# Gate and up products of an expert issued as one pass over two column groups each

## The chip, the cores and the metric

The kernel runs on one core of a Trainium2 chip. TensorE (PE) multiplies, ScalarE (ACT) and VectorE (DVE) do the elementwise work, GpSimd (POOL) helps at the start, and SyncE (SP) issues the transfers, which 16 DMA engines carry out. The metric is the time of one launch on the device, in microseconds (us): the median of the runs, where lower is better.

## The reference

A decoder trunk of two layers on 256 tokens of width 1024, all in float32. Each layer has a mixer (attention and a gated recurrence in layer 0, sliding-window attention in layer 1) and after it a mixture of 32 experts, two of them chosen for each token. The change touches the experts alone, whose arithmetic is:

```python
def expert_block(args):
    xblk, e = args
    hid = jax.nn.silu(xblk @ w_gate[e]) * (xblk @ w_up[e])
    return hid @ w_down[e]
```

`w_gate[e]` and `w_up[e]` are 1024x512, `w_down[e]` is 512x1024: 2 MB each, 6 MB an expert, and every expert's weights are read once in each layer.

## The kernel before

Weights come in chunks of 2 MB (128 partitions x 4096 floats), three to an expert: gate, up, down. Four experts are a quad, so a quad is 12 chunks and a layer 8 quads. The code of a layer's experts is in three pieces: a first quad (`quad(..., first=True)`), a loop over `quad`, and `last_quad`. If more than 32 tokens choose one expert, the loop runs again over all quads.

SBUF has 11 buffers for chunks, seven in `ring` and four in `side`; one of them serves chunk 5 and chunk 11 of a quad. SyncE goes through the chunks in a fixed order (`again`, L357): for each it waits until the chunk that had the buffer has been used (`chunk_done`, which TensorE counts up by one when a product has read its chunk) and then issues the transfer. The last chunk of a layer comes in four pieces (`last_in_pieces`, L387). The queue is first in, first out: later chunks stand behind earlier ones. The mixer's work needs the same buffers, so only the first chunks of a layer's experts are there when its routing ends; the rest start as the first expert gives buffers back (the first chunk's buffer even in three parts, L395).

TensorE works through a quad in one order. It gathers the tokens of the four experts (L989, in the last quad L1169) into `gatherT`, 32 columns an expert. For each expert it then runs the gate product and after it the up product (L1025, in the last quad L1181): the 32 columns of tokens are the stationary operand, the weights move past in four pieces of 128 columns, and the four pieces go to four groups of 32 columns of the array, which run at the same time. So gate lands as 128 partitions x 128 columns of a PSUM bank and up as the next 128 columns. One matmul in float32 is two matmul and two weight-load instructions in the profile: a gate product is 32 matmuls and stands there as x64.

ScalarE waits until gate and up are both done (`products_done(layer, i, 3 * e + 1)` waits for the up chunk) and takes SiLU of the gate part into SBUF (L1556, in the last quad L1568); VectorE multiplies it by the up part (L1656); TensorE turns the result (L1040, L1193); VectorE copies it to SBUF as `hidT` (L2179, L2204); and TensorE runs the down product (L1060, L1202), four steps over `hidT` in four column groups of 256 columns each, x32 in the profile. ScalarE and VectorE copy its result out (L1560 and L2183, L1576).

After a quad TensorE combines the results into the tokens (L1068). In the last quad the combination is done expert by expert (L1092: that of expert 0 stands behind expert 1's up product, that of expert 1 behind expert 2's up product, that of expert 2 behind expert 2's down product), and the fourth expert is followed in small pieces: its gate product, copies of x into PSUM (L1102 in layer 1, L1108 in layer 0), its up product, the rest of these copies, and its down product piece by piece (L1121) as the pieces of the last chunk land.

Of the kernel before, what the change touches and what calls it, by code (L numbers as in the profile page):

```python
# [15 lines left out]
P = 128  # L16
S = 256
TT = S // P
D = 1024
KD = D // P  # L20
# [10 lines left out]
CAP = 32  # L31
QE = 4
# [64 lines left out]
def build(nc, weights, small, table, x_in, xT_in, out):  # L97
# [3 lines left out]
    with ctx:  # L101
# [27 lines left out]
        at = 0  # L129
# [58 lines left out]
        yq = probT[:, 1, :]  # L188
        scr6 = scr[:, :].rearrange("p (b a c) -> p b a c", b=6, a=2)
        silu, hid, hidT = scr6[:, 0, :, :], scr6[:, 1, :, :], scr6[:, 2, :, :]  # L190
        pick, pickw = scr6[:, 3, :, :], scr6[:, 4, :, :]
        pickT = scr[:, 5 * S:6 * S]

# [21 lines left out]
        def last_sums(h, j):  # L215

            return PS[:, LAST[j]:LAST[j] + 2, h * S:(h + 1) * S].rearrange("p j (a n) -> p a j n", a=TT)

        def buffer(n):

# [8 lines left out]
        ident = tb("id")  # L229
# [310 lines left out]
        def _(pe):  # L540
# [461 lines left out]
            def turn_weights(i, layer, bank):  # L1002
# [3 lines left out]
                    tr = pe.transpose(PS[:, bank, t * P:(t + 1) * P], pickw[:, t, :], ident)  # L1006
                tr.then_inc(m_pickw_turned, 1)

            def quad(layer, i, first=False):

                if first:
                    gather_rest(i, layer)
                else:
                    gather(i, layer)
                for e in range(QE):
                    b = 2 + e % 2
                    tok = slice(e * CAP, (e + 1) * CAP)

                    for up in range(2):
                        w = cols(moe_landed(layer, i, 3 * e + up, first))  # L1020
                        for k in range(KD):
                            if e == 0 and up == 0 and k % 4 == 0:
                                pe.wait_ge(m_gatherT, 2 * i + 1 + k // 4)
                            for f in range(4):
                                mm = pe.matmul(PS[f * CAP:(f + 1) * CAP, b, up * P:(up + 1) * P],  # L1025
                                               gatherT[:, k, tok], w[:, k, f * P:(f + 1) * P],
                                               start=(k == 0), stop=(k == KD - 1))
                            if first and e == 0 and up == 0 and k in (1, 3):
                                mm.then_inc(part_read, 1)
                        mm.then_inc(chunk_done, 1)  # L1030
                        if first and e == 0 and up == 0:
                            for t in range(TT):
                                mm = pe.matmul(PS[:, 7, 64:96], tb("ones"), rt[:, 0, t, :], start=(t == 0),
                                               stop=(t == 1))
                            mm.then_inc(counted, 1)
                    if first and e == 0:
                        turn_weights(i, layer, 3)
                        pe.wait_ge(m_pickT, i + 1)
                    pe.wait_ge(m_hid, QE * i + e + 1)
                    pe.transpose(PS[:, b, 2 * P:3 * P], hid[:, e % 2, :], ident).then_inc(m_hid_turned, 1)  # L1040
                    w = halves(moe_landed(layer, i, 3 * e + 2))
                    early = first and e == QE - 1
                    if early:
                        pe.wait_ge(half_landed, 16 * (layer + 1))
                        w0 = spare.rearrange("p (f n) -> p f n", f=4)
                        pe.wait_ge(more_landed, 16 * (layer + 1))

                    def part(f, q):

                        at = f * 512 + q % 2 * 256  # L1050
                        if early and q < 2:
                            return w0[:, f, q * 256:(q + 1) * 256]
                        if early and at < MORE[layer]:
                            return more(layer)[:, at:at + 256]
                        return w[:, q // 2, f, q % 2 * 256:(q % 2 + 1) * 256]

                    pe.wait_ge(m_hidT, QE * i + e + 1)
                    for f in range(4):
                        for q in range(4):
                            mm = pe.matmul(PS[q * CAP:(q + 1) * CAP, e % 2, 0:256],  # L1060
                                           hidT[:, e % 2, f * CAP:(f + 1) * CAP], part(f, q),
                                           start=(f == 0), stop=(f == 3))
                    mm.then_inc(chunk_done, 1)

                pe.wait_ge(m_y, 2 * QE * i + 2 * QE)
                for t in range(TT):
                    for q in range(4):
                        pe.matmul(PS[:, OUT[q], t * 256:(t + 1) * 256], pickT[:, t * P:(t + 1) * P],  # L1068
                                  yq[:, q * 256:(q + 1) * 256], start=(first and t == 0), stop=False,
                                  skip_group_check=True)  # L1070
# [91 lines left out]
            def last_quad(layer, i):  # L1162
# [9 lines left out]
                for e in range(QE):  # L1172
                    b = 2 + e % 2
                    tok = slice(e * CAP, (e + 1) * CAP)
                    for up in range(2):
                        w = cols(moe_landed(layer, i, 3 * e + up))
                        for k in range(KD):
                            if e == 0 and up == 0 and k % 4 == 0:
# [10 lines left out]
                        turn_picks(i)  # L1189
                    elif e < QE - 1:  # L1190
                        combine(i, e - 1)
                    pe.wait_ge(m_hid, QE * i + e + 1)
                    pe.transpose(PS[:, b, 2 * P:3 * P], hid[:, e % 2, :], ident).then_inc(m_hid_turned, 1)  # L1193
                    if e == 0:
                        pe.wait_ge(m_pickT, i + 1)
                    if e == QE - 1:
# [3 lines left out]
                    for f in range(4):  # L1200
                        for q in range(4):
                            mm = pe.matmul(PS[q * CAP:(q + 1) * CAP, e % 2, 0:256],  # L1202
                                           hidT[:, e % 2, f * CAP:(f + 1) * CAP],
                                           w[:, q // 2, f, q % 2 * 256:(q % 2 + 1) * 256],
                                           start=(f == 0), stop=(f == 3))
                    mm.then_inc(chunk_done, 1)
# [90 lines left out]
        def _(act):  # L1297
# [251 lines left out]
                act.wait_ge(chunk_done, DONE_MOE[layer] + j + 1 + QC * i)  # L1549

            def quad(layer, i, weights_bank=2):
                act.wait_ge(m_pickw_turned, i + 1)
                act.activation(pickT[:, :], PS[:, weights_bank, 0:S], ACT.Copy).then_inc(m_pickT, 1)
                for e in range(QE):
                    products_done(layer, i, 3 * e + 1)
                    act.activation(silu[:, e % 2, :], PS[:, 2 + e % 2, 0:P], ACT.Silu).then_inc(m_silu, 1)  # L1556

                    products_done(layer, i, 3 * e + 2)
                    for q in range(2):
# [4 lines left out]
            def last_quad(layer, i):  # L1564

                for e in range(QE):
                    products_done(layer, i, 3 * e + 1)
                    act.activation(silu[:, e % 2, :], PS[:, 2 + e % 2, 0:P], ACT.Silu).then_inc(m_silu, 1)  # L1568
                    if e == 0:
                        act.wait_ge(m_pickw_turned, i + 1)  # L1570
                        act.activation(pickR[:, 0:2, :].rearrange("p e t -> p (e t)"), PS[:, 0, :], ACT.Copy)
# [74 lines left out]
        def _(dve):  # L1646
# [517 lines left out]
            def quad(layer, i, build=None):  # L2164
# [9 lines left out]
                for e in range(QE):  # L2174
                    b = 2 + e % 2
                    dve.wait_ge(m_silu, QE * i + e + 1)
                    tt(hid[:, e % 2, :], silu[:, e % 2, :], PS[:, b, P:2 * P], ALU.mult).then_inc(m_hid, 1)
                    dve.wait_ge(m_hid_turned, QE * i + e + 1)
                    dve.tensor_copy(hidT[:, e % 2, :], PS[:, b, 2 * P:3 * P]).then_inc(m_hidT, 1)  # L2179

# [6 lines left out]
            def last_quad(layer, i):  # L2187
# [5 lines left out]
                for e in range(QE):  # L2193
# [5 lines left out]
                            tt(xs, xs, PS[:, OUT[q], :].rearrange("p (a n) -> p a n", a=TT),  # L2199
                               ALU.add).then_inc(part_acc, 1)  # L2200
                    dve.wait_ge(m_silu, QE * i + e + 1)
                    tt(hid[:, e % 2, :], silu[:, e % 2, :], PS[:, b, P:2 * P], ALU.mult).then_inc(m_hid, 1)
                    dve.wait_ge(m_hid_turned, QE * i + e + 1)
                    dve.tensor_copy(hidT[:, e % 2, :], PS[:, b, 2 * P:3 * P]).then_inc(m_hidT, 1)  # L2204
                for h in range(2):
# [180 lines left out]
```

## Time and profile before

| | us |
|---|---|
| runs | 1134.91, 1135.9, 1137.19 (median 1135.9) |
| profiled execution | 1138.64 |
| its span | 1136.8 |
| TensorE busy in it | 870.0 (77%) |
| VectorE / ScalarE busy | 300.2 / 186.5 |
| mean granted TensorE clock | 0.907 |

The span is from the first to the last instruction of the profiled execution, and 1.84 us of its time lie outside it. That execution took 2.7 us more than the median run. In the profile's 40 slices the experts of layer 0 fill about slices 7 to 21 and those of layer 1 slices 25 to 40; before and between them are the mixers.

### The profile page before, as it was taken

To read this page: it belongs to the slowest core of one execution; us is meant where nothing else is said; L and a number is where in the kernel's file an instruction comes from. 1 tells how busy PE (TensorE), PEld (TensorE's weight loads), DVE (VectorE), ACT (ScalarE), POOL (GpSimd) and SP (SyncE) were. 2 spreads that over 40 slices of the span, in tenths; PEclk is the share of its full clock that TensorE was granted. 3 is DMA by queue.
4 is the path that set the end of the run, shared out by engine and by line. 5 is a ranking of instruction groups with operands and counts; after the bars stand their busy time and mean duration, and the time that the engine had idled before them with its cause. 6 is when DMAs were issued, how large, how long until landed. Compare 5 with 4: busy or idle time off the path is not lost.

```text
span 1136.8 us, 28905 instructions
## 1 busy us (share of the span) xinstructions
PE 870.0 (77%) x12910; PEld 639.2 (56%) x12910; DVE 300.2 (26%) x959; ACT 186.5 (16%) x495; POOL 25.7 (2%) x29
## 2 busy tenths in 40 slices
PE   7999998787575757575779999787776757666666
PEld 6665647676464545454547457576664545444545
DVE  3566735122111111111103774221211111111101
ACT  4323532110000000000003452011100000000000
POOL 1221000000000000000000000000000000000000
PEclk9999999999888879888889999899988888888898
DMA  9955458999999999999999777999999999999997
GB/s 378 430 218 218 164 206 327 416 429 427 432 432 431 429 434 429 429 432 432 427 430 426 302 286 275 381 428 426 432 432 428 432 432 429 431 432 428 431 428 308
DMA packets 34732, 440.91 MB, mean 388 GB/s; under 512 B 3952, under 2 KB 4080, under 8 KB 8048
## 3 DMA queue, kind: packets, MB, share of 16 engines
q1 hardware_dynamic: 34384, 439.89, 92.3%
q8 instruction: 47, 0.77, 0.3%
q10 hardware_dynamic: 288, 0.15, 0.0%
q14 instruction: 13, 0.11, 0.0%
HBM read 438.97 MB, written 1.05 MB: 387 GB/s over the span
## 4 chain that ended last, share of the span: by engine, by line
DMA 52%; PE 37%; DVE 5%; ACT 2%; issue 2%; SPq 1%; DVEq 0%; another core or an unknown queue 0%; ACTq 0%
DMA side<-weights 43%; PE PS L580 9%; DMA ring<-weights 9%; PE PS L1060 8%; PE PS L1025 6%; PE PS L754 1%; PE PS L921 1%; PE PS L590 1%; PE PS L1068 1%; PE PS L989 1%; DVE scr L1656 1%; SPq L357 1%; PE PS L1181 1%; PE PS L665 1%; DVE side L1902 1%
## 5 line engine op out<-in xcount | busy, mean ns | idle before, releaser
L1025 PE MATMUL PS<-ring,probT 128*32 128x128 f32 x4480 | 150.7, 294 | 47.7 <-DMA ring<-weights 43.4
L1025 PEld LDWEIGHTS PS<-ring,probT 128*32 128x32 f32 x4480 | 134.4, 119 | 62.3 <-DMA ring<-weights 51.7
L1025 PE MATMUL PS<-side,probT 128*32 128x128 f32 x2688 | 105.5, 322 | 69.0 <-DMA side<-weights 66.0
L1025 PEld LDWEIGHTS PS<-side,probT 128*32 128x32 f32 x2688 | 92.3, 131 | 88.2 <-DMA side<-weights 81.7
L580 PE MATMUL PS<-ring,side 128*128 128x512 f32 (+1 forms) x320 | 136.2, 575 | 0.3 <-DVE side L1940 0.3
L1656 DVE TENSOR_TENSOR scr<-scr,PS 128x128 f32<-128x128 f32 x64 | 18.5, 288 | 384.9 <-ACT scr L1556 317.4
L580 PEld LDWEIGHTS PS<-ring,side 128*128 128x128 f32 x320 | 58.8, 190 | 61.0 <-issue 59.8
L2183 DVE COPY probT<-PS 32x256 f32<-32x256 f32 x112 | 47.5, 424 | 171.6 <-PE PS L1060 170.8
L1060 PE MATMUL PS<-side,scr 128*32 128x256 f32 x842 | 66.3, 462 | 25.6 <-DMA side<-weights 21.8
L1060 PE MATMUL PS<-ring,scr 128*32 128x256 f32 x896 | 69.1, 460 | 21.9 <-DMA ring<-weights 12.4
L1560 ACT ACTIVATE probT<-PS 32x256 f32<-32x256 f32 x112 | 41.8, 373 | 231.9 <-PE PS L1060 231.3
L1556 ACT ACTIVATE scr<-PS 128x128 f32<-128x128 f32 x56 | 15.5, 277 | 344.7 <-PE PS L1025 344.7
L1068 PE MATMUL PS<-probT,scr 128*128 128x256 f32 x224 | 57.6, 415 | 13.8 <-DVE probT L2183 13.8
L1068 PEld LDWEIGHTS PS<-probT,scr 128*128 128x128 f32 x224 | 45.4, 208 | 30.2 <-DVE probT L2183 23.5
L1060 PEld LDWEIGHTS PS<-ring,scr 128*32 128x32 f32 x896 | 34.7, 127 | 44.7 <-issue 22.1
L1060 PEld LDWEIGHTS PS<-side,scr 128*32 128x32 f32 x842 | 31.3, 127 | 49.0 <-DMA side<-weights 26.7
L1040 PE MATMUL PS<-TB,scr 128*128 128x128 f32 x56 | 19.1, 342 | 42.4 <-DVE scr L1656 42.4
L1656 DVE TENSOR_TENSOR probT<-PS,SM 128x512 f32<-128x512 f32 (+1 forms) x36 | 23.8, 662 | 103.7 <-PE PS L989 88.5
L989 PE MATMUL PS<-scr,x 128*128 128x128 f32 x384 | 46.8, 275 | 0.0
L989 PEld LDWEIGHTS PS<-scr,x 128*128 128x128 f32 x384 | 45.7, 192 | 0.6
L1040 PEld LDWEIGHTS PS<-TB,scr 128*128 128x128 f32 x56 | 8.0, 143 | 59.0 <-DVE scr L1656 56.9
L1181 PE MATMUL PS<-ring,probT 128*32 128x128 f32 x640 | 20.8, 286 | 6.2 <-DMA ring<-weights 5.8
(286 smaller groups left out, 822.1 us busy)
## 6 DMA issues: line engine op xcount, KB each, us to landing
ring<-weights SPq DMA_DIRECT2D x124, 2048.0 KB, 34.1
side<-weights SPq DMA_DIRECT2D x74, 2048.0 KB, 26.9
side<-weights SPq DMA_DIRECT2D x6, 1024.0 KB, 10.2
ring<-weights SPq DMA_DIRECT2D x10, 512.0 KB, 7.3
xn<-weights SPq DMA_DIRECT2D x2, 1024.0 KB, 6.8
ring<-weights SPq DMA_DIRECT2D x2, 1024.0 KB, 8.3
side<-weights SPq DMA_DIRECT2D x5, 256.0 KB, 26.8
xn<-xT_in SPq DMA_DIRECT2D x2, 512.0 KB, 5.5
```

Of the source, the lines that this page charges most:

```text
L357: return sp.dma_start(buffer(slot), source).then_inc(w_landed[slot], 16)
L580: mm = pe.matmul(PS[:, bank, 0:n], hT[:, k, t * P:(t + 1) * P], w[:, k, 0:n], start=(k == 0), stop=(k == KD - 1))
L989: mm = pe.matmul(PS[:, half, k * P:(k + 1) * P], x[:, t, d * P:(d + 1) * P], pick[:, t, :], start=(t == 0), stop=(t == TT - 1))
L1025: mm = pe.matmul(PS[f * CAP:(f + 1) * CAP, b, up * P:(up + 1) * P], gatherT[:, k, tok], w[:, k, f * P:(f + 1) * P], start=(k == 0), stop=( ...
L1040: pe.transpose(PS[:, b, 2 * P:3 * P], hid[:, e % 2, :], ident).then_inc(m_hid_turned, 1)
L1060: mm = pe.matmul(PS[q * CAP:(q + 1) * CAP, e % 2, 0:256], hidT[:, e % 2, f * CAP:(f + 1) * CAP], part(f, q), start=(f == 0), stop=(f == 3))
L1068: pe.matmul(PS[:, OUT[q], t * 256:(t + 1) * 256], pickT[:, t * P:(t + 1) * P], yq[:, q * 256:(q + 1) * 256], start=(first and t == 0), sto ...
L1181: mm = pe.matmul(PS[f * CAP:(f + 1) * CAP, b, up * P:(up + 1) * P], gatherT[:, k, tok], w[:, k, f * P:(f + 1) * P], start=(k == 0), stop=( ...
L1556: act.activation(silu[:, e % 2, :], PS[:, 2 + e % 2, 0:P], ACT.Silu).then_inc(m_silu, 1)
L1560: ins = act.activation(yq[e * CAP:(e + 1) * CAP, q * 256:(q + 1) * 256], PS[q * CAP:(q + 1) * CAP, e % 2, 0:256], ACT.Copy)
L1656: return dve.tensor_tensor(o, a, b, op)
L2183: ins = dve.tensor_copy(yq[e * CAP:(e + 1) * CAP, q * 256:(q + 1) * 256], PS[q * CAP:(q + 1) * CAP, e % 2, 0:256])
```

## The change

An expert's gate and up product become one pass (`gate_up`). The stationary operand and the order over the eight k steps are as before, but a k step has four matmuls of 256 columns in place of eight of 128: gate's 512 columns go to column groups 0 and 1, up's to groups 2 and 3. So the pass waits for both chunks before its first matmul, gate's result lies on partitions 0 to 63 and up's on partitions 64 to 127, each 256 columns wide, and `chunk_done` goes up by two at the end of the pass. SiLU and the multiplication then work on 64 partitions x 256 columns instead of 128x128, the result stands on partitions 64 to 127 (`act_up`), and it is turned by two ordinary matmuls against a 64x64 identity instead of one transpose; the down product reads its four blocks in another order (`hid_rows`). The first expert of a layer's first quad and the last of its last quad keep the old form.

```diff
@@ tiles
+        act_up = scr6[2 * CAP:P, 0:2, :, :].rearrange("p a b c -> p (a b c)").rearrange("p (e n) -> p e n", e=2)
...
+        def hid_rows(f, pair):
+
+            at = (f % 2 * 2 + f // 2 if pair else f) * CAP
+            return slice(at, at + CAP)
...
@@ TensorE
+            def gate_up(layer, i, e, first=False):
+
+                b = 2 + e % 2
+                w = [cols(moe_landed(layer, i, 3 * e + up, first)) for up in range(2)]
+                for k in range(KD):
+                    if e == 0 and k % 4 == 0:
+                        pe.wait_ge(m_gatherT, 2 * i + 1 + k // 4)
+                    for q in range(4):
+                        mm = pe.matmul(PS[q * CAP:(q + 1) * CAP, b, 0:S], gatherT[:, k, e * CAP:(e + 1) * CAP],
+                                       w[q // 2][:, k, q % 2 * S:(q % 2 + 1) * S], start=(k == 0), stop=(k == KD - 1))
+                mm.then_inc(chunk_done, 2)
+
+            def turn_hidden(i, e):
+
+                b = 2 + e % 2
+                pe.wait_ge(m_hid, QE * i + e + 1)
+                for c in range(2):
+                    tr = pe.matmul(PS[:, b, 2 * P + c * 2 * CAP:2 * P + (c + 1) * 2 * CAP],
+                                   act_up[:, e % 2, c * P:(c + 1) * P], ident[2 * CAP:P, 2 * CAP:P],
+                                   start=True, stop=True)
+                tr.then_inc(m_hid_turned, 1)
...
@@ quad, for every expert
-                    for up in range(2):
+                    pair = not (first and e == 0)
+                    if pair:
+                        gate_up(layer, i, e, first)
+                    for up in range(0 if pair else 2):
...
-                    pe.wait_ge(m_hid, QE * i + e + 1)
-                    pe.transpose(PS[:, b, 2 * P:3 * P], hid[:, e % 2, :], ident).then_inc(m_hid_turned, 1)
+                    if pair:
+                        turn_hidden(i, e)
+                    else:
+                        pe.wait_ge(m_hid, QE * i + e + 1)
+                        pe.transpose(PS[:, b, 2 * P:3 * P], hid[:, e % 2, :], ident).then_inc(m_hid_turned, 1)
...
-                                           hidT[:, e % 2, f * CAP:(f + 1) * CAP], part(f, q),
+                                           hidT[:, e % 2, hid_rows(f, pair)], part(f, q),
...
@@ last_quad
-                    for up in range(2):
+                    pair = e < QE - 1
+                    if pair:
+                        gate_up(layer, i, e)
+                    for up in range(0 if pair else 2):
...
@@ ScalarE, quad (last_quad the same, with e == QE - 1 for the old form)
-                    act.activation(silu[:, e % 2, :], PS[:, 2 + e % 2, 0:P], ACT.Silu).then_inc(m_silu, 1)
+                    if first and e == 0:
+                        act.activation(silu[:, e % 2, :], PS[:, 2 + e % 2, 0:P], ACT.Silu).then_inc(m_silu, 1)
+                    else:
+                        act.activation(act_up[:, e % 2, :], PS[0:2 * CAP, 2 + e % 2, 0:S], ACT.Silu).then_inc(m_silu, 1)
...
@@ VectorE, quad (last_quad the same, with e == QE - 1 for the old form)
-                    tt(hid[:, e % 2, :], silu[:, e % 2, :], PS[:, b, P:2 * P], ALU.mult).then_inc(m_hid, 1)
+                    if build is not None and e == 0:
+                        tt(hid[:, e % 2, :], silu[:, e % 2, :], PS[:, b, P:2 * P], ALU.mult).then_inc(m_hid, 1)
+                    else:
+                        tt(act_up[:, e % 2, :], act_up[:, e % 2, :], PS[2 * CAP:P, b, 0:S], ALU.mult).then_inc(m_hid, 1)
```

TensorE in layer 1's last quad, before, from the wait for expert 2's gate chunk to expert 3's gate product. L561 is the wait for a chunk, L1181 the gate and up products, L1089 and L1192 waits, L1092 the combination, L1193 the turn of the hidden block, L1202 the down product:

```order
L561 REGISTER_ALU
L1181 MATMUL PS<-side,probT 32x128 x32
L561 REGISTER_ALU
L1181 MATMUL PS<-ring,probT 32x128 x32
L1089 REGISTER_ALU
L1092 MATMUL PS<-probT,TB 128x256 x8
L1192 REGISTER_ALU
L1193 MATMUL PS<-TB,scr 128x128
L1202 MATMUL PS<-ring,scr 32x256 x16
L1089 REGISTER_ALU
L1092 MATMUL PS<-probT,TB 128x256 x8
L1181 MATMUL PS<-side,probT 32x128 x32
```

The same place now. The two chunk waits stand together at L567, L1023 is the pass over both chunks (the first two of its 16 alternating rows open the first piece, the last two the second), L1126 the combination, L1032 the turn, L1242 the down product, L1218 expert 3's gate product:

```order
L567 REGISTER_ALU x2
L1023 MATMUL PS<-side,probT 32x256 x2
L1023 MATMUL PS<-ring,probT 32x256 x2
```

```order
L1023 MATMUL PS<-side,probT 32x256 x2
L1023 MATMUL PS<-ring,probT 32x256 x2
L1123 REGISTER_ALU
L1126 MATMUL PS<-probT,TB 128x256 x8
L1030 REGISTER_ALU
L1032 MATMUL PS<-TB,scr 128x64 x2
L1242 MATMUL PS<-ring,scr 32x256 x16
L1123 REGISTER_ALU
L1126 MATMUL PS<-probT,TB 128x256 x8
L1218 MATMUL PS<-side,probT 32x128 x32
```

Expert 2's gate product has moved behind the wait for its up chunk; what follows, the combination, the turn, the down product and expert 3, stands in the order it had.

ScalarE in the last quad, before, from expert 2's SiLU to expert 3's (L1568 is the SiLU, L1549 and L1582 wait for products, L1576 copies out a down product):

```order
L1568 ACTIVATE scr<-PS 128x128 [waits chunk_done]
L1549 REGISTER_ALU
L1576 ACTIVATE probT<-PS 128x256 [waits chunk_done]
L1549 REGISTER_ALU
L1568 ACTIVATE scr<-PS 128x128 [waits chunk_done]
L1582 ACTIVATE probT<-PS 128x128 [waits down_half_done]
```

And now (L1615 is the SiLU of the new form, L1613 that of the old):

```order
L1615 ACTIVATE scr<-PS 64x256 [waits chunk_done]
L1589 REGISTER_ALU
L1623 ACTIVATE probT<-PS 128x256 [waits chunk_done]
L1589 REGISTER_ALU
L1613 ACTIVATE scr<-PS 128x128 [waits chunk_done]
L1629 ACTIVATE probT<-PS 128x128 [waits down_half_done]
```

Nothing has moved there; the SiLU of experts 0 to 2 has another shape, and it waited for both products before as well.

## Rows read from the trace of the kernel before

**Rows 1.** The page, busy tenths of the DMA engines in 40 slices
```profile
DMA  9955458999999999999999777999999999999997
```

**Rows 2.** Steady stretches: busy us of each engine (instructions), PEclk, DMA share, GB/s
```profile
262.00:550.00 288.00, 193.47 (x3482) 148.16 (x3478) 41.38 (x110) 22.37 (x65) 0.00 (x0) 0.85 1.01 430
812.00:1070.00 258.00, 168.89 (x3066) 128.36 (x3066) 35.96 (x96) 19.93 (x58) 0.00 (x0) 0.85 1.01 431
```

**Rows 3.** The page, transfers of chunks: count, KB each, median us to landing
```profile
ring<-weights SPq DMA_DIRECT2D x124, 2048.0 KB, 34.1
```

**Rows 4.** TensorE's timeline, layer 0's first quad: start, us, operation
```profile
198.93 3.68 PE L1025 MATMUL PS<-ring,probT 128*32 128x128 f32 x128
```

**Rows 5.** Transfers issued in 198:199.9, and in 200:202: us to landing
```profile
ring<-weights SPq DMA_DIRECT2D x1, 2048.0 KB, 9.1
...
ring<-weights SPq DMA_DIRECT2D x1, 2048.0 KB, 12.3
```

**Rows 6.** SyncE's timeline in layer 1's second quad
```profile
771.51 0.33 SPq L357 DMA_DIRECT2D side<-weights  x1
```

**Rows 7.** The transfer issued in 771.4:771.9: us to landing
```profile
side<-weights SPq DMA_DIRECT2D x1, 2048.0 KB, 11.1
```

**Rows 8.** TensorE's timeline at the end of layer 1
```profile
1105.72 2.73 PE L1181 MATMUL PS<-side,probT 128*32 128x128 f32 x64 [4.33 <-DMA side<-weights]
1110.63 3.35 PE L1181 MATMUL PS<-ring,probT 128*32 128x128 f32 x64 [2.18 <-DMA ring<-weights]
1113.92 1.15 PE L1092 MATMUL PS<-probT,TB 32*128 32x256 f32 x16
1115.80 1.93 PE L1202 MATMUL PS<-ring,scr 128*32 128x256 f32 x32 [0.47 <-DVE scr L2204]
1118.57 1.15 PE L1092 MATMUL PS<-probT,TB 32*128 32x256 f32 x16 [0.83 <-ACT probT L1576]
1120.35 1.96 PE L1181 MATMUL PS<-side,probT 128*32 128x128 f32 x64 [0.63 <-DMA side<-weights]
1122.23 2.86 PE L1102 MATMUL PS<-x,TB 128*128 128x256 f32 x12
1125.18 1.96 PE L1181 MATMUL PS<-side,probT 128*32 128x128 f32 x64
```

**Rows 9.** Weight loads of TensorE there, expert 3's up product
```profile
1125.18 1.69 PEld L1181 LDWEIGHTS PS<-side,probT 128*32 128x32 f32 x64 [0.50 <-DMA side<-weights]
```

**Rows 10.** TensorE's timeline at the end of layer 0
```profile
588.23 1.95 PE L1181 MATMUL PS<-ring,probT 128*32 128x128 f32 x64 [1.24 <-DMA ring<-weights]
...
593.11 1.93 PE L1202 MATMUL PS<-ring,scr 128*32 128x256 f32 x32 [1.59 <-DMA ring<-weights]
...
597.94 3.50 PE L1181 MATMUL PS<-side,probT 128*32 128x128 f32 x64 [1.19 <-DMA side<-weights]
...
604.32 1.96 PE L1181 MATMUL PS<-side,probT 128*32 128x128 f32 x64
```

**Rows 11.** Single microseconds with TensorE's clock, columns as in rows 2
```profile
1112.00:1113.00 1.00, 1.00 (x27) 0.92 (x23) 0.00 (x0) 0.00 (x0) 0.00 (x0) 0.50 0.88 377
```

**Rows 12.** The same in layer 1's first quad
```profile
735.00:736.00 1.00, 1.00 (x22) 0.85 (x14) 0.00 (x0) 0.00 (x0) 0.00 (x0) 0.50 1.11 461
...
740.00:741.00 1.00, 1.00 (x16) 0.53 (x12) 0.00 (x0) 0.00 (x0) 0.00 (x0) 0.50 0.92 393
```

**Rows 13.** Groups by form: count, busy us, mean ns of one, idle before
```profile
L1656 DVE TENSOR_TENSOR scr<-scr,PS 128x128 f32<-128x128 f32 x64 | 18.5, 288 | 384.9 <-ACT scr L1556 317.4 <-ACT scr L1568 67.3
...
L1556 ACT ACTIVATE scr<-PS 128x128 f32<-128x128 f32 x56 | 15.5, 277 | 344.7 <-PE PS L1025 344.7
...
L1656 DVE TENSOR_TENSOR scr<-scr,wexp 128x256 f32<-128x256 f32 x16 | 6.7, 420 | 0.1
...
L1553 ACT ACTIVATE scr<-PS 128x256 f32<-128x256 f32 x14 | 5.4, 383 | 89.3 <-PE PS L1006 89.3
```

**Rows 14.** TensorE's waits over the span: us in total, times, longest
```profile
PE PS L1025 <- issue: 7.2, 5, 2.4
```

More of the change, by code:

```diff
@@ L1191, in last_quad @@
                         combine(i, e - 1)
-                    pe.wait_ge(m_hid, QE * i + e + 1)
-                    pe.transpose(PS[:, b, 2 * P:3 * P], hid[:, e % 2, :], ident).then_inc(m_hid_turned, 1)
+                    if pair:
+                        turn_hidden(i, e)
+                    else:
+                        pe.wait_ge(m_hid, QE * i + e + 1)
+                        pe.transpose(PS[:, b, 2 * P:3 * P], hid[:, e % 2, :], ident).then_inc(m_hid_turned, 1)
                     if e == 0:
@@ L1202, in last_quad @@
                             mm = pe.matmul(PS[q * CAP:(q + 1) * CAP, e % 2, 0:256],
-                                           hidT[:, e % 2, f * CAP:(f + 1) * CAP],
+                                           hidT[:, e % 2, hid_rows(f, pair)],
                                            w[:, q // 2, f, q % 2 * 256:(q % 2 + 1) * 256],
@@ L1551, in quad @@
             def quad(layer, i, weights_bank=2):
+                first = weights_bank == 3
                 act.wait_ge(m_pickw_turned, i + 1)
@@ L1567, in last_quad @@
                     products_done(layer, i, 3 * e + 1)
-                    act.activation(silu[:, e % 2, :], PS[:, 2 + e % 2, 0:P], ACT.Silu).then_inc(m_silu, 1)
+                    if e == QE - 1:
+                        act.activation(silu[:, e % 2, :], PS[:, 2 + e % 2, 0:P], ACT.Silu).then_inc(m_silu, 1)
+                    else:
+                        act.activation(act_up[:, e % 2, :], PS[0:2 * CAP, 2 + e % 2, 0:S], ACT.Silu).then_inc(m_silu, 1)
                     if e == 0:
@@ L2176, in quad @@
                     dve.wait_ge(m_silu, QE * i + e + 1)
-                    tt(hid[:, e % 2, :], silu[:, e % 2, :], PS[:, b, P:2 * P], ALU.mult).then_inc(m_hid, 1)
+                    if build is not None and e == 0:
+                        tt(hid[:, e % 2, :], silu[:, e % 2, :], PS[:, b, P:2 * P], ALU.mult).then_inc(m_hid, 1)
+                    else:
+                        tt(act_up[:, e % 2, :], act_up[:, e % 2, :], PS[2 * CAP:P, b, 0:S], ALU.mult).then_inc(m_hid, 1)
                     dve.wait_ge(m_hid_turned, QE * i + e + 1)
@@ L2201, in last_quad @@
                     dve.wait_ge(m_silu, QE * i + e + 1)
-                    tt(hid[:, e % 2, :], silu[:, e % 2, :], PS[:, b, P:2 * P], ALU.mult).then_inc(m_hid, 1)
+                    if e == QE - 1:
+                        tt(hid[:, e % 2, :], silu[:, e % 2, :], PS[:, b, P:2 * P], ALU.mult).then_inc(m_hid, 1)
+                    else:
+                        tt(act_up[:, e % 2, :], act_up[:, e % 2, :], PS[2 * CAP:P, b, 0:S], ALU.mult).then_inc(m_hid, 1)
                     dve.wait_ge(m_hid_turned, QE * i + e + 1)
```

## The prediction

> **What bounds the kernel now.** I read first the 40 slices of the page, then the two long stretches of the experts, then the transfers, and last TensorE's timeline at the places where a layer's experts begin and end. The DMA row [rows 1] shows 9 in nearly all slices of the experts and gaps only in the mixers. The stretches say the same with a number: DMA share 1.01 at 430 GB/s, while TensorE is busy 193.47 of 288.00 us (67%) and 168.89 of 258.00 us (65%) [rows 2]. A chunk of 2 MB (2.1 million bytes) takes 4.9 us of such a stream, and an expert's three chunks 14.6 us. A chunk is issued 34.1 us before it lands [rows 3], so about seven chunks are in the queue. In the steady stretches the time is that of the stream, and TensorE waits for landings.
>
> So three places can matter: the start of a layer's experts, where the queue is short; the end, where nothing is left to load; and anything that would empty the queue between.
>
> At the end of layer 1 the reader is to see where the waits stop. Expert 2's gate product waits 4.33 us for its chunk, its up product 2.18 us, expert 3's gate product still 0.63 us, and from 1120.35 on TensorE goes from one operation to the next [rows 8]. Expert 3's up product starts at 1125.18, and its weight loads name the landing of its chunk as what they waited for [rows 9], while TensorE came free only at 1122.23 + 2.86 = 1125.09: both arrive within 0.1 us. There is no slack behind expert 3's gate product, so whatever delays it there delays the end of the span by as much.
>
> **The pass itself.** Removed per pair: 128 matmul instructions of 128 columns. Added: 64 of 256 columns. The old pair runs in 3.68 us when both chunks are there [rows 4]. The nearest row for the new form is the down product, which also has 256 columns in each of four groups: 32 instructions in 1.93 us [rows 8], so 64 in at most 3.86. Bounds 3.4 (below the old pair, should the many instructions have cost something) to 3.9; I take 3.7. No TensorE work is saved, the columns are the same.
>
> The Trainium skill (TensorE: Matmul & The Clock Gate, "Wait — 56ns, not 53.3ns?") puts a floor of about 25 ns under each matmul and 2.5 ns on each at full clock. By an estimate from it, 64 instructions fewer would save under 0.2 us of a pair. Rows 4 show 3.68 us / 128 = 29 ns an instruction, near that floor, and rows 8 1.93 / 32 = 60 ns for twice the columns, so the trace shows no such saving.
>
> **What the pair moves.** The gate product no longer runs in the 4.9 us in which the up chunk lands. After the up chunk's landing there are now 3.7 us of work at full clock where there were 1.95. And the clock is not full then. After the waits of this place the granted clock is 0.50 (1.2 of 2.4 GHz) [rows 11], and expert 2's up product takes 3.35 us instead of 1.95 [rows 8]; in layer 0 expert 3's gate product takes 3.50 [rows 10]. TensorE came free of expert 1 at 1105.72 - 4.33 = 1101.4; with expert 1's own pass some 2 us later, it will be idle for about 7 us up to 1110.63, so the pass starts slow. Bounds: 3.7 (full clock) and 7.4 (slow throughout; the clock stayed at 0.50 from 735 to 741 with TensorE mostly busy [rows 12]). A slow stretch in rows 8 and 10 costs one product 1.4 to 1.55 us, so I take one such loss, rounded up for the higher share of slow work: 5.4 us.
>
> **The path behind it, at the end of layer 1.**
> - Expert 2's pass ends at 1110.63 + 5.4 = 1116.0; before, the up product ended at 1113.98. That is +2.0.
> - SiLU waited for both products before too, so it is not newly exposed. It and the multiplication have 256 columns instead of 128: 383 against 277 ns and 420 against 288 ns [rows 13], +0.24 together. They lie beside expert 1's combination of 1.15 us [rows 8], which stands ahead of the turn. SiLU plus multiplication, 0.80 us with some 0.1 of hand-over, still end before it. So 0; without that cover 0.24.
> - The turn by two ordinary matmuls instead of one transpose: no row shows it on 64 partitions. Four instructions of 64 columns against one of 128: from -0.1 to +0.3, taken +0.05.
> - The down product then starts at 1117.9 and not at 1115.80, its copy and expert 2's combination follow as before (1118.57 + 1.15 = 1119.72, now 1121.8). Expert 3's gate product starts at 1121.8 instead of 1120.35. The 0.63 us of its wait have absorbed that part of the shift.
> - Everything behind is the old form and the last pieces are by then landed or about to. The full shift reaches the end: +1.45 us.
>
> **The end of layer 0.** The up chunk of expert 2 is there at 588.23 [rows 10]. The pass ends at 593.6, the down product starts at 595.5 (before 593.11, waiting for its chunk), and expert 3's gate product starts at 599.4 instead of 597.94. But before, it was slow, 3.50 us, after the short waits of 1.59 and 1.19 us. Now TensorE runs through from 588.23 with hardly a wait, so I take full clock: it ends at 601.35 instead of 601.44. The up product at 604.32 was already later than its chunk, because TensorE came late. So -0.1 here, with bounds of -1.6 (pass at full clock) and +1.5 (pass slow throughout).
>
> **The start of a layer.** The first expert is in the old form, so the stream restarts when it did. Expert 1's gate chunk gives its buffer back about 1.8 us later, at the end of the pass. Behind it waits SyncE's next load. The load issued at the end of expert 0's down product, 199.1, landed 9.1 us later at 208.2; the next, issued at the end of the gate product at about 200.9, landed at 213.2 [rows 5], 5 us behind, so it stood in the queue until 208.2. A delay of 1.8 us is hidden by 7 us of queue. TensorE is the later one in this stretch, so its small additions (0.24 + 0.05 us a pair) sum up: five pairs, 1.5 us, until layer 1's second quad frees a buffer at 771.51 [rows 6]. That load landed at 782.6 [rows 7], its own transfer took 4.9, so it began at 777.7: more than 6 us of queue against 1.5. Cost 0; if that cover were gone, up to 2 us.
>
> **In the loop.** After the up chunk the pass may end 1 to 3 us later than the up product did. That is far below the 14.6 us to the next expert's up chunk, and the seven chunks in the queue hide the later return of the gate buffers. 0.
>
> **Sum.** +1.45 - 0.1 = +1.35 us on the profiled execution of 1138.64 us (span 1136.8, 1.84 outside it). That execution was 2.7 us above the median. On the median of 1135.9 it is 1137.2 us, +0.12%. What a measurement can tell from no change is 0.2%, 2.3 us.
>
> **Rivals.**
> - *Slow clock through the whole pass (slower).* At both ends the pass takes 7.4 us and not 5.4. Layer 1 then loses 1.45 + 2.0 = 3.45, layer 0 up to 1.5: +4.9, 1140.8 us. For it speaks that the low clock lasted some 6 us in rows 12; against it that in rows 8 the first product after the slow one, L1092, takes its full-speed 1.15. It decides once the pass takes over 6.2 us. Chance 0.20. The Trainium skill (TensorE: Matmul & The Clock Gate, Part 1) says that the count of slow matmuls at the start of a burst varies from run to run; the two unequal ends in rows 8 and 10 agree.
> - *A stall of TensorE's own instruction supply falls into the end (slower).* The trace has five idle times before L1025 that no other engine explains, 7.2 us in sum, 2.4 the longest [rows 14]. They come after long runs without a wait, and expert 2's pass starts such a run up to the end. One of them there gives +3.7, 1139.6 us. Against it: half the matmul instructions of a pass are gone. Chance 0.08. By the Trainium skill (Runtime: NRT & Kernel Launch, "Instruction fetch mechanics") fetching is hidden in straight code, which would make this 0; rows 14 speak against that.
> - *Full clock (no change or slightly faster).* The pass takes 3.7 us at both ends: 1110.63 + 3.7 = 1114.3, expert 3's gate product is ready at 1120.1 and waits for its chunk as before, and layer 0 gains 1.6. 1134.3 us. Against it the slow 3.35 us of rows 8. Chance 0.12.
> - *The queue runs dry at a start (slower).* +2 on top, 1139.2 us. Rows 5 to 7 speak against it. Chance 0.03.
> - *The stream itself gets faster, from fewer instruction and weight reads.* Nothing shows it: the DMA share is 1.01 in both stretches with TensorE at 65 and 67%. With over 0.2% it would be 1133 us. Chance 0.07.
>
> **How the numbers follow.** The forecast has 0.50, with its own range of 1135.5 to 1138.6. Of it some 0.06 lies above 1138.2, 0.01 below 1133.6. Slower: 0.20 less a little that stays within the bound, 0.08, 0.03 and 0.06 give 0.34. Faster: 0.07, and a small part of the full-clock case, 0.10. Same: 0.56. The range goes to the slow-clock case above and to the full-clock case below: 1134.0 to 1140.6.
>
> **What would show it.** The chunk of expert 2's up product lands where it did, and its pass takes about 5.4 us, starting at granted clock 0.50. Expert 3's gate product in layer 1 has no wait for a DMA ahead of it and starts about 1.5 us later against its chunk; in layer 0 it takes 1.96 us and not 3.50. DMA share in the long stretches stays 1.01, and TensorE's busy time changes by less than 3%. Wrong would be a wait of the up product of expert 3 for its chunk in layer 1 (then the stream moved, not TensorE), a drop of the DMA share in the first two quads, or a pass under 3.4 us.

## The result and the profile after

| | us |
|---|---|
| before, 9 runs | 1136.22 (1133.98 to 1137.44) |
| changed, 9 runs | 1139.75 (1137.76 to 1141.32) |
| ratio | 1.0035, 95% interval 1.0023 to 1.0047 |
| changed, on another occasion beside three experiments, 10 runs | ratio 1.0034 (1.0019 to 1.0049) |
| profiled execution of the changed kernel | 1140.06, span 1138.3 |

The change makes the kernel 3.5 us slower. The forecast was 1.35 us more, so direction and range held, and the size was too small. The forecast's largest chance, 0.56, stood on a change under 2.3 us either way; the 0.34 for a slower kernel was the case that came.

The DMA row of the page after the change, which answers to [rows 1], and then the two long stretches, which answer to [rows 2] (busy us and instructions of PE, PEld, DVE, ACT, POOL, then clock, DMA share, GB/s):

```profile
DMA  9955458999999999999999768999999999999995
```

```profile
262.00:550.00 288.00, 201.77 (x2234) 128.40 (x2236) 43.23 (x108) 23.58 (x63) 0.00 (x0) 0.82 1.01 431
812.00:1070.00 258.00, 170.41 (x1965) 106.66 (x1965) 37.28 (x93) 20.96 (x56) 0.00 (x0) 0.85 1.01 431
```

The stream is what it was: share 1.01, 431 against 430 GB/s. TensorE has over a third fewer matmul records and is no less busy: it moves the same columns. Over the whole span it is busy 879.3 us instead of 870.0, 1.1% more.

TensorE's timeline at the end of layer 1 after the change, which answers to [rows 8]. The pass over expert 2's two chunks (L1023) is many alternating records; its first and last are shown:

```profile
1108.20 0.64 PE L1023 MATMUL PS<-side,probT 128*32 128x256 f32 x2 [8.36 <-DMA ring<-weights]
...
1113.52 0.38 PE L1023 MATMUL PS<-ring,probT 128*32 128x256 f32 x2
1113.83 1.15 PE L1126 MATMUL PS<-probT,TB 32*128 32x256 f32 x16
1114.91 0.66 PE L1032 MATMUL PS<-TB,scr 64*128 64x64 f32 x4
1116.04 1.93 PE L1242 MATMUL PS<-ring,scr 128*32 128x256 f32 x32 [0.47 <-DVE scr L2257]
1118.81 1.15 PE L1126 MATMUL PS<-probT,TB 32*128 32x256 f32 x16 [0.83 <-ACT probT L1623]
1119.88 1.95 PE L1218 MATMUL PS<-side,probT 128*32 128x128 f32 x64
...
1124.69 1.95 PE L1218 MATMUL PS<-side,probT 128*32 128x128 f32 x64
```

Two executions can't be laid over each other by their clock times, because the stream runs up to 3.5 us earlier or later from one to the next: expert 2's up product or pass begins 397.3 to 400.8 us after layer 0's first gate product in the profiles of this study. Count from the start of the product that waits for expert 2's up chunk. Before, expert 3's gate product started 1120.35 - 1110.63 = 9.72 us behind it, after a wait for its own chunk. Now it starts 1119.88 - 1108.20 = 11.68 us behind, with no wait. That is +1.96 us. The pass itself takes 1113.52 + 0.38 - 1108.20 = 5.70 us. Expert 3's up product, at 1124.69, has no wait for its chunk either.

A record of two matmuls takes 0.64 us at first and 0.38 us in the end: the pass begins on the low clock. Single microseconds inside it, columns as above, say so:

```profile
1109.00:1110.00 1.00, 1.00 (x16) 0.48 (x12) 0.00 (x0) 0.00 (x0) 0.00 (x0) 0.50 0.92 393
1113.00:1114.00 1.00, 1.00 (x24) 0.41 (x16) 0.00 (x0) 0.02 (x1) 0.00 (x0) 1.00 1.03 442
```

At the end of layer 0, which answers to [rows 10]:

```profile
585.32 0.64 PE L1023 MATMUL PS<-side,probT 128*32 128x256 f32 x2 [7.68 <-DMA ring<-weights]
...
591.26 1.15 PE L1126 MATMUL PS<-probT,TB 32*128 32x256 f32 x16
...
597.03 1.96 PE L1218 MATMUL PS<-side,probT 128*32 128x128 f32 x64
```

The pass takes 6.0 us there, 585.32 to about 591.3, and the gate product of expert 3 takes 1.96 us. Where both chunks are there and the clock is full, one record shows the whole pass (expert 1's, the same last quad):

```profile
569.91 3.66 PE L1023 MATMUL PS<-ring,probT 128*32 128x256 f32 x64 [1.12 <-DMA ring<-weights]
```

### The profile page after: what moved, and what is told of

Read it like the earlier page. It is cut to its first block, busy times and chain, and to the rows that moved or that the text cites. A ratio compares the mean times of both kernels' runs of the same rounds, so it can differ in the third digit from the quotient of the medians.

```text
span 1138.3 us, 21622 instructions
## 1 busy us (share of the span) xinstructions
PE 879.3 (77%) x9250; PEld 578.0 (51%) x9250; DVE 308.3 (27%) x959; ACT 192.4 (17%) x495; POOL 25.6 (2%) x29
## 4 chain that ended last, share of the span: by engine, by line
DMA 47%; PE 40%; DVE 6%; ACT 3%; issue 2%; SPq 2%; DVEq 0%; ACTq 0%
DMA side<-weights 41%; PE PS L1023 10%; PE PS L586 9%; DMA ring<-weights 6%; PE PS L1094 5%; SPq L363 2%; PE PS L1032 1%; PE PS L760 1%; DVE scr L1703 1%; PE PS L927 1%; PE PS L596 1%; ACT scr L1600 1%; PE PS L671 1%; DVE side L1949 1%; DVE side L1703 1%
## 5 line engine op out<-in xcount | busy, mean ns | idle before, releaser
L1023 PE MATMUL PS<-side,probT 128*32 128x256 f32 x1408 | 152.0, 486 | 115.7 <-DMA ring<-weights 67.5
L1023 PE MATMUL PS<-ring,probT 128*32 128x256 f32 x2432 | 201.1, 423 | 20.6 <-DMA ring<-weights 20.6
L1023 PEld LDWEIGHTS PS<-side,probT 128*32 128x32 f32 x1408 | 80.3, 139 | 185.5 <-issue 129.3
L1023 PEld LDWEIGHTS PS<-ring,probT 128*32 128x32 f32 x2432 | 107.7, 121 | 65.5 <-issue 36.1
L1703 DVE TENSOR_TENSOR scr<-scr,PS 64x256 f32<-64x256 f32 (+1 forms) x64 | 26.6, 416 | 388.4 <-ACT scr L1600 324.6
L1032 PE MATMUL PS<-TB,scr 64*128 64x64 f32 x240 | 39.3, 284 | 51.3 <-DVE scr L1703 51.3
L1600 ACT ACTIVATE scr<-PS 64x256 f32<-64x256 f32 x54 | 20.3, 375 | 346.6 <-PE PS L1023 346.6
L1032 PEld LDWEIGHTS PS<-TB,scr 64*128 64x128 f32 x240 | 31.0, 186 | 79.0 <-DVE scr L1703 78.6
L1094 PEld LDWEIGHTS PS<-side,scr 128*32 128x32 f32 x842 | 34.5, 122 | 30.1 <-issue 19.5
L2229 DVE COPY scr<-PS 128x128 f32<-128x128 f32 x56 | 16.3, 292 | 41.3 <-PE PS L1032 40.3
```

The lines of the kernel that those rows point to most:

```text
L1023: mm = pe.matmul(PS[q * CAP:(q + 1) * CAP, b, 0:S], gatherT[:, k, e * CAP:(e + 1) * CAP], w[q // 2][:, k, q % 2 * S:(q % 2 + 1) * S], star ...
L1032: tr = pe.matmul(PS[:, b, 2 * P + c * 2 * CAP:2 * P + (c + 1) * 2 * CAP], act_up[:, e % 2, c * P:(c + 1) * P], ident[2 * CAP:P, 2 * CAP:P] ...
L1094: mm = pe.matmul(PS[q * CAP:(q + 1) * CAP, e % 2, 0:256], hidT[:, e % 2, hid_rows(f, pair)], part(f, q), start=(f == 0), stop=(f == 3))
L1600: act.activation(act_up[:, e % 2, :], PS[0:2 * CAP, 2 + e % 2, 0:S], ACT.Silu).then_inc(m_silu, 1)
L1703: return dve.tensor_tensor(o, a, b, op)
```

## The experiments

All kernels are the changed one with the set of experts chosen that use the new form. A table near the top names them, and the loops ask it ("the ends" are the last quads of the two layers):

```diff
+PAIRED = {"first": (1, 2, 3), "loop": (0, 1, 2, 3), "last": (0, 1, 2)}
...
-                    pair = e < QE - 1
+                    pair = e in PAIRED["last"]
```

| run | first quads | loop | last quads | median us | ratio to before (95%) |
|---|---|---|---|---|---|
| changed_again | 1, 2, 3 | all | 0, 1, 2 | 1139.68 | 1.0034 (1.0019 to 1.0049) |
| only_end | none | none | 0, 1, 2 | 1139.91 | 1.0028 (1.0016 to 1.0041) |
| only_e2 | none | none | 2 | 1140.98 | 1.0048 (1.0030 to 1.0066) |
| no_e2 | 1, 2, 3 | all | 0, 1 | 1134.75 | 0.9986 (0.9973 to 0.9999) |
| old_end | 1, 2, 3 | all | none | 1133.68 | 0.9984 (0.9972 to 0.9997) |
| old_end_again | 1, 2, 3 | all | none | 1135.16 | 0.9988 (0.9975 to 1.0001) |
| warm_pass | 1, 2, 3 | all | 0, 1, 2 + 8 matmuls | 1133.24 | 0.9984 (0.9971 to 0.9996) |
| warm_pass_again | the same | | | 1134.61 | 0.9986 (0.9976 to 0.9996) |
| only_loop | none | all | none | 1135.18 | 0.9992 (0.9983 to 1.0001) |
| only_first | 1, 2, 3 | none | none | 1136.00 | 1.0005 (0.9995 to 1.0014) |
| old_end_warm | 1, 2, 3 | all | none + 3 matmuls | 1136.44 | 1.0009 (0.9996 to 1.0022) |
| before_warm | none | none | none + 3 matmuls | 1134.79 | 1.0002 (0.9990 to 1.0014) |

Each ratio is to runs of the kernel before made on the same occasion. Their median was 1136.53 us beside old_end, only_end, only_e2 and warm_pass, 1135.73 beside only_loop, only_first, old_end_warm and before_warm, and 1136.81 beside the other four.

**Where the loss is made.** The first theory was that it is made at the ends, by the pass of expert 2. The rival was that the later return of the gate buffers in the first quads and the loop costs the stream something.

```diff
-"last": (0, 1, 2)
+"last": ()
```

> The new form in the first quads and in the loop as in the changed kernel, the old form for all four experts of both last quads. Theory 1 (the loss is made at the two ends, by expert 2's pass that starts when its up chunk lands and mostly on the low clock): all of the loss is gone, 1136.2 us (ratio to before 1.000), and expert 3's gate product in layer 1 waits for its chunk again. Theory 2 (the loss is made where the new form frees the gate buffers later, in the first quads and the loop): nothing is regained, 1139.7 us (1.003).

Measured 0.9984: the loss is gone, and more. The wait of expert 3's gate product in layer 1 did not come back in this profile, where expert 2's down product took 3.39 us on the low clock; it did in old_end_again (0.92 us) and in no_e2 below.

```diff
-"first": (1, 2, 3), "loop": (0, 1, 2, 3)
+"first": (), "loop": ()
```

> The new form for experts 0 to 2 of the two last quads alone, the old form everywhere else. Theory 1: the whole loss is there, 1139.2 to 1139.8 us (1.003). Theory 2: none of it, 1136.2 us (1.000).

Measured 1.0028, the loss with none of the rest. The rival falls. The next kernel is this one with fewer experts:

```diff
-"last": (0, 1, 2)
+"last": (2,)
```

> The new form for expert 2 of the two last quads alone. Theory 1 puts the loss on this one pass: 1139.2 to 1139.8 us (1.003), as with all three. If the passes of experts 0 and 1 matter, because they end later and leave the low clock differently, 1137 to 1138 us (1.001 to 1.0015). Theory 2: 1136.2 us (1.000).

Measured 1.0048 with this one pass in each layer, more than the 1.003 expected, though the interval, of 7 runs, reaches down to 1.0030. Part of the excess is in the profile, where the pass in layer 1 takes 6.55 us; the rest is not explained. The counterpart is the changed kernel with only this pass taken back:

```diff
-"last": (0, 1, 2)
+"last": (0, 1)
```

> The changed kernel with the old form for expert 2 of the last quads too, so that only experts 0 and 1 of them are paired. Theory 1 (the loss is expert 2's pass alone): like the kernel with four old experts at the ends, 0.998 to 1.000 of before, 1133.7 to 1136.2 us. If experts 0 and 1 have a part in the loss: 1.001 to 1.002.

Measured 0.9986. The loss is expert 2's pass; those of experts 0 and 1 cost nothing that can be measured. The same place at the end of layer 1 in this kernel:

```profile
1099.45 1.96 PE L1219 MATMUL PS<-side,probT 128*32 128x128 f32 x64 [2.77 <-DMA side<-weights]
1104.33 3.18 PE L1219 MATMUL PS<-ring,probT 128*32 128x128 f32 x64 [2.93 <-DMA ring<-weights]
...
1114.05 1.96 PE L1219 MATMUL PS<-side,probT 128*32 128x128 f32 x64 [0.42 <-DMA side<-weights]
```

Expert 2's gate product is done while the up chunk lands, and expert 3's waits for its chunk again, 9.72 us behind the up product as before.

**Is it the low clock?** The changed kernel with work added ahead of that pass:

```diff
                     pair = e in PAIRED["last"]
+                    if e == QE - 2:
+                        moe_landed(layer, i, 3 * e)
+                        for n in range(8):
+                            pe.matmul(PS[:, b, 0:S], ident, TB[:, 0:S], start=True, stop=True)
```

> The changed kernel with eight matmuls of 256 columns added in both last quads, issued when expert 2's gate chunk has landed, ahead of its pass; they write into the PSUM columns that the pass then overwrites. They keep TensorE at work up to the landing of the up chunk. Theory 1: the pass takes 3.7 us instead of 5.6 to 6.0; the end of layer 1 gets 1.7 us back and layer 0 about 1.5, so 1136.4 to 1137.0 us (1.000 to 1.001), and expert 3's gate product in layer 1 starts within 0.4 us of its chunk. If the low clock is not what costs (the doubled work behind the landing is), 1139 us (1.0025).

Measured 0.9984, 0.5% below the changed kernel and more than expected. Its timeline at the end of layer 1 (L1214 are the added matmuls), and the pass behind them as one stretch (columns as above):

```profile
1099.53 5.10 PE L1214 MATMUL PS<-TB 128*128 128x256 f32 x16 [2.82 <-DMA side<-weights]
...
1108.15 1.15 PE L1127 MATMUL PS<-probT,TB 32*128 32x256 f32 x16
...
1114.20 1.96 PE L1223 MATMUL PS<-side,probT 128*32 128x128 f32 x64
```

```profile
1104.60:1108.20 3.60, 3.60 (x69) 1.99 (x68) 0.00 (x0) 0.00 (x0) 0.00 (x0) 1.00 1.01 432
```

The pass runs at clock 1.00 from 1104.6 to 1108.2, 3.67 us where it took 5.70. With the full clock the loss is gone, though the doubled work behind the landing is still there: at full clock TensorE is done with it about when expert 3's gate chunk lands, 9.64 us behind the start of the pass.

Not all of the 0.5% is the clock. The two profiles of the changed kernel also have a final store that is 1.3 to 2.0 us longer than in any of the other twelve, this one among them (see the part on the prediction). The two ends taken by themselves, in the table there, show the clock's part: 20.13 and 20.10 us here, 22.27 and 22.14 in the changed kernel.

> The changed kernel with the eight matmuls ahead of expert 2's pass, as run once before at 0.9984. Theory 1 puts it level with the kernel with old ends, whatever that comes to: within 0.001 of it, and 0.003 to 0.005 below the changed kernel.

Measured 0.9986, beside 0.9988 for old ends and 1.0034 for the changed kernel. In layer 1 of its profile expert 3's gate chunk landed late and its product then ran on the low clock, after a pass at full clock:

```profile
1117.31 3.33 PE L1223 MATMUL PS<-side,probT 128*32 128x128 f32 x64 [1.35 <-DMA side<-weights]
```

> The changed kernel itself, on this chip beside the three others: 1.0035 again if the loss is the same here, at least 1.0023.

**Does the new form gain anything away from the ends?** The first kernels without the slow pass stood 0.16% below before. Parts of the new form alone:

```diff
-"first": (1, 2, 3), "last": (0, 1, 2)
+"first": (), "last": ()
```

> The new form for all experts of the loop's quads, the old form in the first and the last quads. The kernel with the old ends and the new form elsewhere took 0.9984 of before (0.9972 to 0.9997). Theory A (the loop's passes gain it): 0.9984 again, 1134.4 us. Theory B (the gain comes from the first quads, where TensorE ran out of instructions in the old form): 1.000, 1136.2 us. Theory C (there is no gain, 0.9984 was chance): 1.000.

```diff
-"loop": (0, 1, 2, 3), "last": (0, 1, 2)
+"loop": (), "last": ()
```

> The new form for experts 1 to 3 of the two first quads alone. Theory A: 1.000, 1136.2 us. Theory B: 0.9984, 1134.4 us. Theory C: 1.000. In all of them TensorE's idle times without a releaser before the gate and up products of the first quads go from some 4 us to under 1.

Measured 0.9992 and 1.0005, both with 1 inside the interval. Theory B falls, A expected 0.9984 for the first, and C, no gain, is not excluded. In only_first the idle times without a releaser are gone from the first quads, where before had 4.8 us of them, as expected; 5.7 us of such times stand in its second quads instead. The repetition:

> The kernel with the old form at the ends and the new form elsewhere, as run once before at 0.9984 (0.9972 to 0.9997). The new form in the loop alone gave 0.9992, in the first quads alone 1.0005, and this kernel with three matmuls more 1.0009. If the new form away from the ends gains something: 0.998 to 0.999 again. If it was chance: 0.9995 to 1.0005.

0.9988 is in the range expected of a gain, with 1.0001 at the end of its interval. Two runs of the kernel with old ends, one of its neighbour without expert 2's pass and two with the added matmuls all lie at 0.9984 to 0.9988. They are less than five signs, since they share two sets of runs of before (1136.53 and 1136.81); beside the third set (1135.73) no kernel came under 0.9992, and old_end_warm below, which has the same new form away from the ends, came to 1.0009. A gain of some 1.5 us away from the ends is possible, not shown, and its cause is open.

**Two attempts to gain at expert 3's gate product.** Before, it took 3.50 us on the low clock in layer 0 [rows 10]. Three matmuls fill TensorE's wait there:

```diff
                     if e == QE - 2:
+                        pe.matmul(PS[:, b, 0:S], ident, TB[:, 0:S], start=True, stop=True)
                         combine(i, e)
+                        for n in range(2):
+                            pe.matmul(PS[:, b, 0:S], ident, TB[:, 0:S], start=True, stop=True)
```

> The new form in the first quads and the loop, the old form in the last quads, and three added matmuls of 256 columns in each last quad between expert 2's down product and expert 3's gate product (one ahead of expert 2's combination, two behind it), which fill TensorE's wait there. If expert 3's gate product on the low clock costs anything (3.50 us in layer 0 before), it takes 1.96 us and the kernel gains up to 1.5 us on the one with the old ends: 1132.7 to 1134 us (0.997 to 0.998). If that product is on the low clock only now and then, 1134.4 (0.9984).

> The kernel before with the same three added matmuls in each last quad and nothing of the change. If the low clock at expert 3's gate product costs it: 0.999 (up to 1.4 us less). If not: 1.000, with at most 0.4 us more where the added matmuls end after the landing.

Measured 1.0009 and 1.0002: nothing gained, against 0.997 to 0.998 and 0.999 expected. The product took 1.96 us in both profiles, but it does in nearly all the others too (below), so there was little to gain. The three matmuls also seem to end after the landing: in before_warm the product starts 10.02 and 10.29 us behind expert 2's up product, without a wait, where it waits and starts 9.72 us behind in before.

## Why the prediction was too small

Two times can be read in each of the 14 profiles. First, at both ends, from the start of the product or pass that reads expert 2's up chunk to the start of the last part of expert 3's down product. Second, from there to the end of the span, in layer 1. Single executions, so each number carries the chance of where a chunk lands:

| kernel | expert 2 at the ends | layer 0, us | layer 1, us | last part to end |
|---|---|---|---|---|
| before | old | 21.75 | 20.20 | 5.97 |
| only_loop | old | 20.24 | 20.19 | 6.03 |
| only_first | old | 20.23 | 20.20 | 5.97 |
| no_e2 | old | 20.21 | 20.20 | 5.97 |
| old_end | old | 20.23 | 20.61 | 6.02 |
| old_end_again | old | 21.79 | 20.87 | 5.98 |
| old_end_warm | old | 21.57 | 20.91 | 6.03 |
| before_warm | old | 20.43 | 21.45 | 6.01 |
| mean of these eight | | 20.81 | 20.58 | |
| changed | new | 22.27 | 22.14 | 7.96 |
| changed_again | new | 22.36 | 21.98 | 7.28 |
| only_end | new | 21.60 | 22.08 | 6.03 |
| only_e2 | new | 22.03 | 22.98 | 6.06 |
| mean of these four | | 22.07 | 22.30 | |
| warm_pass | new, full clock | 20.13 | 20.10 | 6.04 |
| warm_pass_again | new, full clock | 20.13 | 22.99 | 6.05 |

The 22.99 is the late chunk and the slow gate product of expert 3 shown above. Among the old ones, 21.75 holds the slow gate product of [rows 10], and 21.79 and 21.57 other delays behind the up product.

**The start, the loop, the stream: right.** The costs of 0 held. The kernels with the new form there and not at the ends stand at 0.9984 to 1.0009 of before, and the DMA share stayed 1.01.

**The pass: right, a little too small.** 5.7 and 6.0 us for 5.4; in the eight such passes of the four kernels it takes 5.35 to 6.55. At full clock it takes 3.66 for 3.7, against 3.68 of the old pair [rows 4]. Half the instructions save nothing.

**The end of layer 1: right, somewhat too small.** The means give 22.30 - 20.58 = +1.72, the two profiles first compared 22.14 - 20.20 = +1.94; the forecast was +1.45. The pass took 0.3 us more than forecast. The turn of the hidden block takes 0.66 us for its four instructions, where the old one took 0.33; the forecast added 0.05 and had 0.3 as the bound.

**The end of layer 0: the step that failed.** The forecast let the new form gain 1.55 us there, because expert 3's gate product had run on the low clock for 3.50 us [rows 10], and put the end at -0.1. The means give 22.07 - 20.81 = +1.26. Against that one profile the gain did come: 22.27 - 21.75 = +0.52. But in the other seven kernels with the old form for expert 2 that gate product takes 1.95 or 1.96 us at both ends, as it did in layer 1 before. The 3.50 us are an exception, met once more in the 3.33 us of warm_pass_again, and the execution that had them was 2.7 us over its median. The gain was credited to the new form in full, and most executions do not have it to give. A slip of 0.25 us in the working made the forecast a little better than its own steps: expert 2's combination ended at 596.76 before, 3.65 us behind the start of its down product, so 595.5 leads to 599.15 for expert 3's gate product and not to 599.4, and the end of layer 0 would have stood at -0.35. So the two ends cost 1.26 + 1.72 = 3.0 us and not 1.35.

**A part that no step had.** The two profiles of the changed kernel take 7.96 and 7.28 us from the last part to the end, the other twelve 5.97 to 6.06. The two output transfers take longer to land. The rows are of before from 1131.4 on, and of the changed kernel from 1128 on (count, KB each, median us to landing), with the rates of the changed kernel in 40 slices of 1128 to the end:

```profile
out<-x SPq DMA_DIRECT2D x2, 512.0 KB, 2.7
```

```profile
GB/s 0 0 0 0 0 0 0 0 0 0 0 0 0 0 0 273 425 410 364 372 38 182 402 387 379 440 106 30 23 23 30 23 23 15 0 0 0 0 0 30
...
out<-x SPq DMA_DIRECT2D x2, 512.0 KB, 4.4
```

For its last 1.8 us the store moves 15 to 30 GB/s, about a sixteenth of its rate before, as if one of the 16 DMA engines were behind. In the microsecond from 1132.3, inside this store, the changed kernel has this packet of instructions (packets, MB, share of 16 engines), and changed_again this one from 1131.5:

```profile
q8 instruction: 1, 0.02, 11.3%
```

```profile
q8 instruction: 1, 0.02, 7.7%
```

The shares are 0.113 x 16 = 1.8 and 0.077 x 16 = 1.2 us of one engine, and the two stores are longer by 1.95 and 1.27 us. In all twelve others the last such packet starts 6 us or more before the end of the span, ahead of the store, which is issued 5.1 us before it in the kernel before. So 1.3 to 2.0 us of the changed kernel's time goes with where its code is cut into such packets. Store and packet go together in 14 of 14 profiles, and the sizes agree in both that have it; that the packet is the cause was not tried by itself.

**The sum.** 3.0 at the ends and 1.3 to 2.0 in the store make 4.3 to 5.0 us. The changed kernel stands 1139.68 - 1135.16 = 4.5 us above the kernel with old ends that ran beside it, by the ratios 0.46% or 5.2 us. Against before the loss is 3.5 us; the rest would be a gain of the new form away from the ends, which the runs neither show nor exclude. only_end, whose store is the usual one, has the ends alone: 3.0 us would be 1.0026, and 1.0028 was measured.

That the range held is in part luck. It reached up to 1140.6 for a slow clock through the whole pass, and the measured time came there by a gain in layer 0 that was not there to be had and by a store that no step priced.

**The rivals.** The low clock through the whole pass, 7.4 us, did not happen in the two profiles of the changed kernel; only_e2 passes the mark of 6.2 us in layer 1, with 6.55 from 1109.86 to 1116.41. A stall of TensorE's instruction supply at the end did not happen in the changed kernel either: its matmuls have no idle time without a releaser, where [rows 14] had 7.2 us. Such idle time does stand at the ends of kernels with old ends: old_end has it for 3.7 us in all in layer 1's last quad, 1.78 of them inside expert 2's gate product (its up product then starts without a wait), old_end_again for 4.4 us over both layers' last quads. Both are still at 0.9984 and 0.9988, so times of this kind ahead of the last waits cost nothing that can be seen. At the start their absence gained nothing measurable (only_first, 1.0005).

## What to carry to other kernels

Where a stream of weights is the bound, as here, TensorE's work counts only behind the last landings, and a form that waits for two chunks before it starts puts the first one's work there, on a clock that the wait has lowered: keep the old form there, or keep TensorE at work, for the last expert and also for the one before it. Before a term credits a change with removing a slow step, look for that step at the places that should behave alike; in one profiled execution it may be an exception. And where an edit moves the program text, look at the last transfers too before the whole difference is put down to the edit.

## What the runs showed of the hardware

- Eight matmuls that compute nothing needed, ahead of the pass, took it from 5.7 and 6.0 us down to 3.67 at both ends.
- 64 matmul instructions of 256 columns in four column groups take 3.66 us and 128 of 128 columns 3.68 us, both at full clock: the columns count, and the number of instructions makes no difference here.
- A packet of instructions that falls into the final store goes with 1.3 to 2.0 us more for it, about the time that the packet takes of one engine (1.2 and 1.8 us). Such packets move with the code: the last one starts from 5.3 to 10.3 us before the end of the span in the 14 profiles.
- Turning a block by four instructions of 64 columns on 64 partitions takes 0.66 us, by one of 128 columns 0.33.
- Five runs without the slow pass (old_end twice, no_e2, warm_pass twice) stand at 0.9984 to 0.9988 of before. One of the five intervals reaches past 1, and the five share two sets of runs of before.
